# Two of the four gate heads' products of layer 0 issued among the first products of panel 2

## The reference, cut to what matters

```python
def gla_mixer(u, w_in, w_gk2, b_gk2, o_norm, w_out):      # u: normed x, (1, 512, 1024)
    proj = u @ w_in                                        # 3088 columns
    q, k, v, gk_lr, g = jnp.split(proj, [512, 1024, 2048, 2064], axis=-1)
    gk = jax.nn.log_sigmoid((gk_lr @ w_gk2 + b_gk2).astype(jnp.float32)) / GATE_NORMALIZER
    ...                                                    # 4 heads, 128 features of q, k and gk each
    b = jnp.cumsum(gk, axis=3)                             # inside chunks of 64 tokens
    q_dec = q * jnp.exp(b)
    k_inv = k * jnp.exp(-b)
    ...
```

## Time and profile before

| | |
|---|---|
| median of three runs | 1137.76 us (1137.74 to 1138.15) |
| the profiled execution's own time | 1139.88 us |
| its span, first to last instruction | 1138.1 us |
| mean granted TensorE clock over the span | 0.98 |
| TensorE matmuls busy | 1075.7 us (95%) |
| VectorE, ScalarE, GpSimd busy | 510.8, 282.7, 264.3 us |

### The profile page before, as it was taken

One profiled execution on the slowest core, in us unless ns is written; L12 is line 12 of the kernel. 1 busy time (PEld: TensorE's weight loads), 2 busy tenths in 40 slices (PEclk: granted clock), 3 DMA queues, 4 the chain that ended last, 5 costly groups with the idle time before them and its releaser, 6 DMA issues.

```text
span 1138.1 us, 17940 instructions
## 1 busy us (share of the span) xinstructions
PE 1075.7 (95%) x7465; PEld 646.8 (57%) x7465; DVE 510.8 (45%) x961; ACT 282.7 (25%) x461; POOL 264.3 (23%) x373
## 2 busy tenths in 40 slices
PE   6999999998999999996999999999989999999991
PEld 5688887873444434442788877777844444344430
DVE  3465237545532344326423347764365432344317
ACT  4442344320000000004232227663210000000012
POOL 1200012004334433223000013340023334433131
PEclk9899999999999999997999999999999999999996
DMA  9443312258999999998223220004179999999965
GB/s 323 125 147 111 110 38 74 99 198 333 404 420 421 422 423 423 422 419 295 95 82 111 74 74 1 1 1 162 51 302 417 416 420 421 423 423 423 422 228 199
DMA packets 68699, 283.24 MB, mean 249 GB/s; under 512 B 15048, under 2 KB 15216, under 8 KB 44064
## 3 DMA queue, kind: packets, MB, share of 16 engines
q1 hardware_dynamic: 47440, 239.32, 52.5%
q0 software_dynamic: 15232, 38.69, 9.4%
q10 hardware_dynamic: 5968, 4.40, 1.2%
HBM read 259.96 MB, written 22.41 MB: 248 GB/s over the span
## 4 chain that ended last, share of the span: by engine, by line
PE 84%; DVE 6%; POOL 3%; issue 3%; DMA 3%; ACT 1%; POOLq 0%; DVEq 0%
PE ps L1850 44%; PE ps L1517 11%; PE ps L1518 10%; PE ps L1519 10%; POOL xn_r L2303 1%; PE ps L1749 1%; DMA xn<-output_table,pos 1%; DVE h L1391 1%; PE ps L2064 1%; PE ps L1527 1%; DVE xn_r L1442 1%; DMA pad<-normed_rows,token 1%; PE ps L1661 1%; PE ps L1739 1%; PE ps L1684 1%
## 5 line engine op out<-in xcount | busy, mean ns | idle before, releaser
L1850 PE MATMUL ps<-raw,s_f 128*32 128x256 f32 (+1 forms) x1536 | 177.1, 456 | 1.3 <-DVE s_f L1209 1.3
L1850 PE MATMUL ps<-w_f,s_f 128*32 128x256 f32 (+1 forms) x1536 | 172.9, 451 | 1.8 <-issue 1.8
L1850 PE MATMUL ps<-xT_f,s_f 128*32 128x256 f32 (+1 forms) x1344 | 149.8, 451 | 0.0
L1223 DVE TENSOR_TENSOR pad<-pad,ps 128x256 f32<-128x256 f32 x32 | 13.5, 421 | 297.3 <-ACT pad L791 297.3
L1850 PEld LDWEIGHTS ps<-raw,s_f 128*32 128x32 f32 (+1 forms) x1536 | 68.1, 120 | 104.5 <-issue 84.1
L1850 PEld LDWEIGHTS ps<-w_f,s_f 128*32 128x32 f32 (+1 forms) x1536 | 69.3, 119 | 94.1 <-issue 71.9
L1850 PEld LDWEIGHTS ps<-xT_f,s_f 128*32 128x32 f32 (+1 forms) x1344 | 59.9, 119 | 92.2 <-issue 75.2
L940 DVE SCALAR_TENSOR_TENSOR w_lo<-raw,gainT,w_hi 128x512 fp32r<-128x512 f32 x88 | 60.1, 746 | 105.5 <-ACT w_hi L595 105.5
L1233 DVE STREAM_TRANSPOSE s_f<-pad 32x128 f32<-32x128 f32 x256 | 103.1, 403 | 4.1
L1517 PE MATMUL ps<-w_hi,xT_hi 128*128 128x512 f32 x240 | 98.0, 408 | 6.0 <-DVE w_lo L940 3.0
L2260 POOL DMA_DIRECT2D output_table<-pad x60 | 33.7, 566 | 291.3 <-ACT pad L797 280.8
(11 more groups left out here) (299 smaller groups left out, 1467.5 us busy)
## 6 DMA issues: line engine op xcount, KB each, us to landing
raw<-in_m_w_down SPq DMA_DIRECT2D x28, 1024.0 KB
w_f<-in_m_w_down SPq DMA_DIRECT2D x28, 1024.0 KB
xT_f<-in_m_w_gate SPq DMA_DIRECT2D x26, 1024.0 KB
xT_f<-in_m_w_up SPq DMA_DIRECT2D x26, 1024.0 KB
raw<-in_m_w_gate SPq DMA_DIRECT2D x18, 1024.0 KB
raw<-in_m_w_up SPq DMA_DIRECT2D x18, 1024.0 KB
w_f<-in_m_w_gate SPq DMA_DIRECT2D x18, 1024.0 KB
w_f<-in_m_w_up SPq DMA_DIRECT2D x18, 1024.0 KB
```

Source lines behind the costliest of these rows:

```text
L1223: ve.tensor_tensor(hid2[:, 0:2 * P], sil2[:, 0:2 * P], ps[:, 0, 2 * P:4 * P], ALU.mult)
L1850: ins = te.matmul(ps[rows * n:rows * (n + 1), bank + kind, 0:width // parts], stationary(k, kind), weights(k, parts, n), start=k == 0, sto ...
```

## The change

Heads 0 and 1 stay where they were. Heads 2 and 3 are issued inside `dense(2, 2, True)`: head 2 behind the three matmuls of the first output tile (k = 0, j = 0), head 3 behind those of the second (k = 0, j = 1). The wait for `panel_out` 1, and the wait for the split of block 2 inside `dense`, thus stand ahead of heads 2 and 3. `gates_done` is set behind head 3. The operands and the banks are the same, and no matmul is added or taken away.

```diff
-            def dense(p, c, feature_major, middle=lambda: None):
+            def dense(p, c, feature_major, middle=lambda: None, behind=lambda k, j: None):
...
                             ins = three(o, *ops, start=k == 0, stop=k == KT - 1)
+                            behind(k, j)
                     ins.then_inc(M["blk_used"], 1)
...
             pe.wait_ge(V["lr_ready"], 3)
-            for i in range(GH):
+
+            def gate_head(i):
                 ins = te.matmul(ps[:, 4 + i, :], wgk2[:, DK * i:DK * (i + 1)], lrT, start=True, stop=True)
-            ins.then_inc(M["gates_done"], 1)
+                if i == GH - 1:
+                    ins.then_inc(M["gates_done"], 1)
+
+            def late_heads(k, j):
+                if k == 0 and j < 2:
+                    gate_head(j + 2)
+
+            gate_head(0)
+            gate_head(1)
             pe.wait_ge(A["panel_out"], 1)
-            dense(2, 2, True)
+            dense(2, 2, True, behind=late_heads)
             pe.wait_ge(V["gates_in"], GH)
```

## The result

The changed kernel is slower: ratio 1.0042, 95% interval 1.0027 to 1.0056 (median 1142.93 us of 8 runs, 1140.38 to 1145.84; before 1137.75 us of 8 runs, 1136.61 to 1140.47). That is 4.8 us (3.1 to 6.4) on 1137.75 us. The forecast was 3.2 us slower, 1141.0 us, with a range of 1138.8 to 1142.6 us. By the ratio the changed kernel takes 1142.5 us, just inside the upper end of that range; the median itself lies 0.3 us above it.

What follows compares the result with a forecast made beforehand. TensorE was taken as the bound (84% of the span). Idle 0.9 us, transitions 0.5 us and 1.8 us for 4.0 us more at the lower clock made 3.2 us, added to 1137.76 us: 1141.0 us, range 1138.8 to 1142.6 us.

Steps and rivals of the forecast that it cites:

- The wait that shows: After heads 0 and 1, TensorE idles 1.0 us until 47.7 us for panel_out; 0.9 us of the summed loss.
- The turns: Switches between products and heads 2 and 3 in panel 2: two more entries and two more returns, 0.5 us.
- The fall: Under the heads, TensorE's granted clock drops to 0.50 at 47.6 us as before, so all that follows starts at 1.2 GHz.
- The rise: In panel 2 the clock returns between 57.4 and 59.6 us, taken as 58.5 us, after dense products start at 54.6 us.
- The later gates: VectorE gets the gates 5.1 us later, hidden behind panel 2 with 3 to 4 us to spare.
- Further on: From panel 2 to the experts the 3.2 us pass unchanged; nothing added for later stretches at the lower clock.
- A: Main case: clock falls at 47.6 us, rises between 57.4 and 59.6 us; 1140.5 to 1141.5 us; chance 0.58.
- D: Clock rises later, at 61 to 62 us, or a later low-clock stretch is lengthened too; 1142.4 us; chance 0.11.
- B: Clock stays at 2.4 GHz as panel 2 begins; 1.8 us gained, 1136.0 us; chance 0.08.
- C: Clock rises at 54.5 us in panel 2, as before; 1.4 us lost, 1139.2 us; chance 0.13.
- E: Loss is taken up further on, such as by the experts' weight stream; no change, 1137.8 us; chance 0.07.
- F: Late gates become the bound, TensorE waiting ahead of panel 3; over 1142 us; chance 0.03.

Runs made afterwards that it cites:

- e6: Changed kernel, but each panel 2 group of output tile j waits for bank j alone; ratio 1.0002 (0.9984 to 1.0020) to the kernel before.
- e2: Kernel before with the wait for emptied banks 0 to 3 moved ahead of heads 2 and 3, nothing interleaved; ratio 1.0017 (1.0004 to 1.0030).
- e4: Changed kernel with heads of 128 rows instead of 16, the gate product left out; ratio 1.0005 (0.9992 to 1.0018) to the kernel before.
- e3: Kernel before with heads of 128 rows instead of 16, the gate product left out; ratio 0.9988 (0.9974 to 1.0002).
- e5: Changed kernel run again unaltered, for a second trace; ratio 1.0031 (1.0014 to 1.0049) to the kernel before.
- e12: Kernel before run again unaltered, for a second trace; one run, 1141.21 us.
- e1: Kernel before with only the gates_done signal later, behind 12 products of panel 2; ratio 1.0007 (0.9997 to 1.0017).
- e9: Changed kernel with heads 2 and 3 behind the first two groups of k = 2; ratio 1.0057 (1.0034 to 1.0080) to the kernel before.
- e7: Changed kernel with bank-by-bank waits, only head 0 ahead, heads 1, 2, 3 behind groups 0, 1, 2; ratio 1.0011 (0.9994 to 1.0028) to before.
- e11: Kernel before with its four heads on four groups of 32 rows, plus bank-by-bank waits for panel 2; ratio 0.9973 (0.9958 to 0.9988).

## Why the prediction was right, point by point

**The wait that shows: right.** Heads 0 and 1 done, TensorE stood until L688 had ended. Forecast 0.9 us, by e6 0.7 us, by e2 1.2 us.

**The turns: right, a little low.** Forecast 0.5 us for two heads, by e6 0.8 us. A head at the lower clock took 2.0 us where 1.85 us was forecast; the return cost 0.73 us as forecast. Together with the wait 1.4 us were forecast, and 1.5 us (27.2 against 25.7 us) measured. The 1.3 us of e4 against e3 do not bear on the turns, as heads of 128 rows had none.

**The fall: later than forecast.** I kept it at 47.6 us. It came 4.0 us behind the heads' start instead of 2.7 us, so the first group still ran at 2.4 GHz.

**The rise: a little late.** Dense products ran from 55.1 us and the clock rose at 60.3 us, 5.2 us later (5.4 us in e5), just outside the bounds of 2.8 to 5.0 us. Since the fall too was late, the stretch was 3.4 us longer than before's; 4.0 us was forecast.

**The sum in one trace: right, and closer than its terms.** 3.15 us (e5 less before 3.2 us, e5 less e12 3.3 us) against 3.2 us. The later fall worked against the later rise and the dearer turns. That they cancel to 0.1 us is luck.

**The sum over the runs: low by 1.6 us, in e5 by 0.3 us.** Two terms can hold this. The first is "1.8 us of 4.0 us more at the lower clock". It takes before's 6.9 us at the lower clock as what every run pays, and e1's trace has none of it with the same order on TensorE. The second is that I added nothing for later stretches at the lower clock. The two pairs of traces have 3.2 us more in the segment, as forecast, and 1.2 us more behind it. The mean granted clock, which every run lists, gives the size of both together: the time lost to the clock is 26.0 us over the 8 runs of the changed kernel and 25.2 us over the 12 of e5, against 22.2 and 22.8 us over two sets of 35 runs of before. That is 2.4 to 3.8 us for the clock where 1.8 us was forecast (it counts the whole span, also where TensorE sets nothing). With 1.5 us for wait and turns it makes 3.9 to 5.3 us, against 4.8 and 3.5 us by the two ratios. How the excess splits between the two terms stays open.

**The later gates: right.** In the changed kernel the split of block 4 ends at 70.93 + 2.72 = 73.65 us, 4.7 us ahead of L988, where 3 to 4 us were forecast. That is owed to the long stretch at the lower clock: in e4, with the clock up, it is 2.2 us (70.31 against 72.50 us), and e1's signal, later still against its panel, used up the cover. e9 brings the gates 4.8 us later still (59.90 against 55.14 us, with the heads begun at the same 46.06 us), and its panel 2, with less low clock, is through 3.2 us earlier; TensorE waits 3.4 us.

**Further on: right that nothing takes the loss up.** The measured times hold all of it, and more: see the two terms above. The 0.9 us more on the way to the experts in the first trace are within what two traces of before differ by (189.2 and 190.4 us).

**The rivals.** A has the mechanism of the segment, but the time came out above its 1140.5 to 1141.5 us. 1142.5 us is what D gave (1142.4 us), for a clock that rises later or a later stretch that is lengthened too. The rise was 0.2 to 0.4 us past A's bound and the traces have more low clock further on, so a part of D came true. e5's ratio, on 1137.76 us, is 1141.3 us and within A. B (clock stays up) is refuted for the traced runs and may be what happens in a part of the runs, by the clock of the lower four of e5; no trace of such a run was taken. C is refuted for the traced runs, E by both ratios. F is real, as e9 shows, but the change's own lateness does not reach it.

What stays open is what decides whether the clock falls under the heads. Neither the row count (e3 against before) nor full products between the heads (e7) settled it.

## What to carry to other kernels

Work on TensorE that stands between a panel and a wait for its banks is cover; moving it behind the wait lays the wait bare, and each 16-row head set among full products costs some 0.4 us by itself, where one of 128 rows cost nothing. The wait can also bring time at the lower clock with it, more than it costs itself: without it (e6) the changed order was level with before. If such small matmuls hurt, run them at the same time and let the next panel wait bank by bank, as e11 does, 3.1 us faster than before. And a single trace shows one course of the clock: before a term is taken from a stretch at the lower clock, compare it with a second trace of the same kernel, or with the mean granted clock of all its runs.

## What the runs showed of the hardware

Four heads of 16 rows on four row groups took 1.14 us for eight records where one after another took 3.70 us, at the same clock. A 32-bit head of 16 rows among full products cost 0.2 us on its way in and 0.2 us on the first product behind it at 2.4 GHz; one of 128 rows cost neither (e1, e6 against e3, e4). The course of the clock under the same order of TensorE's instructions differed from execution to execution (0, 6.8 and 6.8 us at the lower clock in the traces of e1, before and e12). Unaltered, the kernel before took from 1134.4 to 1141.7 us over 35 runs on one chip, far more than the 0.4 us that its first three runs had shown.
